# Three buffers for S1 in the seven-product matmul of a two-block layer, its loads and sums issued ahead, and S4 summed onto S2 in place

## The chip, the core and the metric

One core of a Trainium2 chip runs the whole program once. The time is device time in microseconds (us) of that one launch. TensorE is written PE, VectorE DVE, ScalarE ACT, GpSimd POOL, SyncE SP. SP and POOL issue the transfers that this text speaks of: SP the plain loads, POOL the loads that add onto what is in the buffer (an accumulating transfer), and the stores of the sigmoids.

## What is computed

A pooling block is followed by a layer with three attention branches. The change touches only two products of it: the gate logits (three matrices of 2048 x 2048, of which 42 of 48 tiles of 128 outputs are made in this way) and the last product with `w_out` (14 of its 16 tiles).

```python
def hybrid_layer(x, mem, ..., w_out):
    hn = rms_norm_2(x, norm_gain)
    proj = hn @ w_in                       # its last 3 * 2048 columns are gate_logits
    ...
    g = jax.nn.sigmoid(gate_logits.reshape(b, s, N_BRANCHES, D_MODEL))
    y = g[:, :, 0] * ua + g[:, :, 1] * ub + g[:, :, 2] * uc
    return x + y @ w_out
```

There are 512 tokens and 2048 features, all in float32.

## The kernel before

All activations lie feature by feature (128 partitions) with 512 tokens along the row. A float32 product is made of float32r parts: a weight tile is rounded to a high part by ACT (`pw_hi`, line 1496) and DVE takes the rest (`pw_lo`, line 2017); PE then multiplies high by high, high by low and low by high.

**Pairs.** The two stages that the change touches work on *pairs*: two output tiles of 128 features together. The weights of a pair are a 2 x 2 block matrix (two output tiles by the even and the odd feature tiles), and instead of eight block products seven are made (a Strassen-Winograd scheme), with these seven factors in this order:

| step o | factor | where it comes from |
|---|---|---|
| 0 | A11 | loaded by SP (line 985) |
| 1 | A12 | loaded by SP (line 997) |
| 2 | S2 | DVE: S1 + A11 (line 2028) |
| 3 | S1 | block (1,0) loaded by SP, the *base* (line 991), block (1,1) added onto it by a POOL transfer, the *sum* (line 2376) |
| 4 | S3 | base loaded by SP (line 1003), block (0,0) added by POOL (line 2381) |
| 5 | S4 | DVE: S2 + A12 (line 2031) |
| 6 | A22 | loaded by SP (line 1009) |

Each factor is 128 x 1024 float32, 512 KB, and has one buffer of 4 KB a partition in the space of `x3`. Seven of the eight such places are in use. One product (a step) is 16 matmuls, eight of 512 columns (line 1190) and eight of 256 (line 1192). There are 21 pairs for the gates (pairs 0 to 20, the *gate stage*) and 7 for the output (pairs 21 to 27, the *output stage*), with the attention and branch stages between.

**What sets the order.** Every engine's program is written out by hand and waits on semaphores. PE goes through the steps in order and waits at each for `pw_lo_ready`. ACT (`act_product`) and DVE (`dve_product`) work two steps ahead of PE: at step l, ACT and DVE convert the factor of step l+2, as the three buffers of `pw_hi` and `pw_lo` allow. DVE also makes the sums S2 and S4 four steps ahead (`weight_sum(f.ahead(4))`): at step 5 of a pair it adds one finished product (`added`), makes S2 of the *next* pair, and only then the low part of the next pair's A11:

```python
if f.o == 5:
    added(f, fifth_term, 3, chain[f.j])
    weight_sum(f.ahead(4))       # S2 of the next pair: waits s1_summed
...
factor_lo(f.ahead(2))            # A11 of the next pair
```

SP loads the factors of the next pair in the order A11, S1, A12, S3, A22, each when its single buffer has been read: S1 after `pw_lo` of the present pair's S1 (step 3, done by DVE at step 1), A12 after the present pair's S4 sum, S3 after `pw_lo` of S3. POOL does for each pair a sigmoid store, the sum onto S1, another sigmoid store, the sum onto S3, in that order (`gate_pair`). In the output stage POOL does only the two sums, and SP also loads `x_back` between the factors (`back_load`).

Of the kernel before, what the change touches and what calls it, by code (L numbers as in the profile page):

```python
# [6 lines left out]
F32 = mybir.dt.float32  # L7
# [5 lines left out]
P = 128  # L13
# [143 lines left out]
def program(nc, stream, wmod, cvec, xT, memT, cols_in, const_in, dist_in, x_store, c_store, mkv_store, sig_store, silu_store, out):  # L157
    ctx = ExitStack()
    with ctx:
# [13 lines left out]
        def sb(name, shape, dt, at):  # L173
# [20 lines left out]

        a11, s1, a12, s3, a22, s2, s4 = [sb(f"factor_{name}", [P, 8 * P], F32, at_x3 + 4 * KB * n) for n, name in
                                         enumerate(("a11", "s1", "a12", "s3", "a22", "s2", "s4"))]

# [710 lines left out]
        def _(sp):  # L908
# [66 lines left out]
            def load_factors(pair, which):  # L975

                first = pair.i is None and pair.c in (0, PAIRS)
                tiles = KT // 2 if pair.c == PAIRS else 0
                if "a11" in which:
                    if first:  # L980
                        sp.wait_ge(t_ready, tiles + 1)
                    else:
                        sp.wait_ge(pw_lo_ready, ((pair - 1).times(7) + 1).value())
                        sp.wait_ge(w_sum_made, (pair.times(2) - 1).value())
                    sp.dma_start(a11[:, :], block_in_stream(pair, 0, 0)).then_inc(a11_loaded, 16)
                if "s1" in which:
                    if first:
                        sp.wait_ge(t_ready, tiles + 2)
                    else:
                        sp.wait_ge(pw_lo_ready, ((pair - 1).times(7) + 4).value())  # L990
                    sp.dma_start(s1[:, :], block_in_stream(pair, 1, 0)).then_inc(s1_loaded, 16)
                if "a12" in which:
                    if first:
                        sp.wait_ge(t_ready, tiles + 3)
                    else:
                        sp.wait_ge(w_sum_made, pair.times(2).value())
                    sp.dma_start(a12[:, :], block_in_stream(pair, 0, 1)).then_inc(a12_loaded, 16)
                if "s3" in which:
                    if first:
                        sp.wait_ge(t_ready, tiles + 4)  # L1000
                    else:
                        sp.wait_ge(pw_lo_ready, ((pair - 1).times(7) + 5).value())
                    sp.dma_start(s3[:, :], block_in_stream(pair, 1, 0)).then_inc(s3_loaded, 16)
                if "a22" in which:
                    if first:
                        sp.wait_ge(t_ready, tiles + 5)
                    else:
                        sp.wait_ge(pw_lo_ready, ((pair - 1).times(7) + 7).value())
                    sp.dma_start(a22[:, :], block_in_stream(pair, 1, 1)).then_inc(a22_loaded, 16)
            every = ("a11", "s1", "a12", "s3", "a22")  # L1010
            load_factors(At(0), every)
            with steps(sp, 1, PAIRS) as i:
                load_factors(At(0, 1, i), every)
            sp.wait_ge(product_done, PRODUCTS - 2)
# [35 lines left out]
            for n in range(2):  # L1050
                back_load(n)
            load_factors(At(PAIRS), every)
            sp.wait_ge(xp_stored, 16 * (KT - 2))
            for p in range(OUT_PAIRS):
# [3 lines left out]
                if p + 1 < OUT_PAIRS:  # L1058
                    load_factors(At(PAIRS + p + 1), ("s1", "a12"))
                back_load(3 + 2 * p)  # L1060
                if p + 1 < OUT_PAIRS:
                    load_factors(At(PAIRS + p + 1), ("s3", "a22"))


# [180 lines left out]
        def _(act):  # L1245
# [227 lines left out]
            def factor_hi(f):  # L1473
# [19 lines left out]
                if (f.n - 2).positive():  # L1493
                    act.wait_ge(product_done, (f.n - 2).value())
                source = (a11, a12, s2, s1, s3, s4, a22)[f.o]
                nc.scalar.activation(pw_hi[f.slot][:, :], source[:, :], ACT.Copy).then_inc(pw_hi_ready, 1)  # L1496
# [177 lines left out]
        def _(dve):  # L1674
# [335 lines left out]
            def factor_lo(f):  # L2010

                dve.drain()
                if f is None:
                    return
                source = (a11, a12, s2, s1, s3, s4, a22)[f.o]
                dve.wait_ge(pw_hi_ready, (f.n + 1).value())
# [3 lines left out]
            def weight_sum(f):  # L2020
# [4 lines left out]
                if f.o == 2:  # L2025
                    dve.wait_ge(a11_loaded, once)
                    dve.wait_ge(s1_summed, once)
                    nc.vector.tensor_tensor(s2[:, :], s1[:, :], a11[:, :], ALU.add).then_inc(w_sum_made, 1)  # L2028
                else:
                    dve.wait_ge(a12_loaded, once)  # L2030
                    nc.vector.tensor_tensor(s4[:, :], s2[:, :], a12[:, :], ALU.add).then_inc(w_sum_made, 1)  # L2031

# [296 lines left out]
        def _(pool):  # L2329
# [43 lines left out]
            def sum_s1(pair):  # L2373

                pool.wait_ge(s1_loaded, (pair + 1).times(16).value())
                pool.dma_start(s1[:, :], block_in_stream(pair, 1, 1), accum_op=ALU.add).then_inc(s1_summed, 16)

# [5 lines left out]
            def gate_pair(q, i=None, sums=True):  # L2383

                pair = At(q, 3, i)
                if q or i:
                    n, b = At(2 + 2 * ((q - 1) // 3), 2, i), (q - 1) % 3
                    sigmoid_store(pair.times(2) + 1, n, b, 0)
                if sums:
                    sum_s1(pair + 1)  # L2390
                if q or i:
                    sigmoid_store(pair.times(2) + 2, n + 1, b, 1)
# [148 lines left out]
```

## Time and profile before

| | us |
|---|---|
| median of 3 runs (lowest to highest) | 2201.09 (2198.33 to 2208.2) |
| the profiled execution | 2200.44 |
| its span in the trace | 2198.9 |
| PE busy in the span | 2118.8 |
| DVE busy | 1594.6 |
| ACT busy | 972.5 |
| POOL busy | 126.4 |
| DVE's waits before S2 for the transfers of S1, 26 in all | 83.8 |
| PE's waits for `pw_lo`, 26 in all | 47.2 |

The profiled execution lies 0.65 us under the median of the runs, so what is read from the trace can be taken off the median as it stands. The ends of matmuls are modelled, and they overlap; how long a product takes is read from the start of its first matmul to the start of the next product's.

### The profile page before, as it was taken

What the parts mean: (1) busy time and instruction counts of PE and PEld (TensorE: products, weight loads), DVE (VectorE), ACT (ScalarE), POOL (GpSimd) and SP (SyncE); (2) the same over time, 40 slices, a digit from 0 to 9 for tenths busy, and PEclk for the clock granted to TensorE, in tenths of its full rate; (3) what the DMA queues carried; (4) which work ended last, traced back from release to release, by engine and by line L of the source; (5) the groups of instructions that cost most, each with busy time, mean ns of one, the idle gap of its engine ahead of it and who ended that gap; (6) DMA issues with size and microseconds to landing.
All of it is one profiled execution on the core that took longest, in us unless ns stands there. A gap on an engine that the chain in (4) does not pass through costs nothing.

```text
span 2198.9 us, 32924 instructions
## 1 busy us (share of the span) xinstructions
PE 2118.8 (96%) x10600; PEld 1758.8 (80%) x10600; DVE 1594.6 (73%) x2685; ACT 972.5 (44%) x1664; POOL 126.4 (6%) x201
## 2 busy tenths in 40 slices
PE   7899999999999899999999999999999999999898
PEld 6788887888887777777778878888787888888787
DVE  6888877675658677767676666666778776777676
ACT  6434454333335444444454444444545444224343
POOL 0000000000000111111110000000000000000000
PEclk9999999999999999999999999999999999999999
DMA  9767422655544667676764222222222224665775
GB/s 377 278 213 272 141 96 95 238 207 183 164 149 148 186 175 200 186 208 176 208 162 132 87 88 94 86 87 86 68 87 69 92 90 134 209 217 188 205 211 162
DMA packets 98026, 354.72 MB, mean 161 GB/s; under 512 B 11109, under 2 KB 13557, under 8 KB 89601
## 3 DMA queue, kind: packets, MB, share of 16 engines
q1 hardware_dynamic: 75600, 272.92, 37.4%
q0 software_dynamic: 19584, 76.04, 13.4%
q10 hardware_dynamic: 2738, 4.47, 0.5%
q8 instruction: 53, 0.87, 0.2%
q14 instruction: 51, 0.42, 0.1%
HBM read 328.45 MB, written 24.94 MB: 161 GB/s over the span
## 4 chain that ended last, share of the span: by engine, by line
PE 58%; DMA 15%; DVE 15%; DVEq 5%; ACT 4%; issue 3%; ACTq 0%; SPq 0%; POOLq 0%; POOL 0%
PE bank L427 18%; PE bank L429 17%; PE bank L428 17%; DMA factor_s<-stream 13%; DVE pw_lo L2017 5%; DVE w_lo L421 2%; PE bank L1190 2%; DVE factor_s L2028 1%; DVE factor_s L2031 1%; ACT w_hi L411 1%; PE bank L552 1%; PE bank L583 1%; DVEq L416 1%; DMA front_raw<-stream 1%; DVEq L2085 1%
## 5 line engine op out<-in xcount | busy, mean ns | idle before, releaser
L427 PE MATMUL bank<-x,w_hi 128*128 128x512 f32 x2000 | 789.4, 395 | 3.6 <-ACTq L1376 1.2
L429 PE MATMUL bank<-x,w_lo 128*128 128x512 f32 x2000 | 778.9, 389 | 0.0
L428 PE MATMUL bank<-x,w_hi 128*128 128x512 f32 x2000 | 778.8, 389 | 0.0
L1190 PE MATMUL bank<-x,pw_hi 128*128 128x512 f32 x1568 | 564.7, 404 | 51.1 <-DVE pw_lo L2017 47.2
L421 DVE TENSOR_TENSOR w_lo<-w_raw,w_hi 128x512 fp32r<-128x512 f32 x468 | 324.0, 692 | 315.6 <-ACT w_hi L411 284.2
L411 ACT ACTIVATE w_hi<-w_raw 128x512 fp32r<-128x512 f32 x468 | 295.9, 632 | 577.0 <-PE bank L429 475.6
L427 PEld LDWEIGHTS bank<-x,w_hi 128*128 128x128 f32 x2000 | 375.4, 188 | 95.5 <-issue 8.8
L1192 PE MATMUL bank<-x,pw_lo 128*128 128x256 f32 x1568 | 443.5, 283 | 0.0
L429 PEld LDWEIGHTS bank<-x,w_lo 128*128 128x128 f32 x2000 | 375.4, 188 | 79.7
L428 PEld LDWEIGHTS bank<-x,w_hi 128*128 128x128 f32 x2000 | 375.7, 188 | 75.3 <-issue 0.2
L1190 PEld LDWEIGHTS bank<-x,pw_hi 128*128 128x128 f32 x1568 | 300.0, 191 | 131.3 <-issue 30.7
L1192 PEld LDWEIGHTS bank<-x,pw_lo 128*128 128x128 f32 x1568 | 301.5, 192 | 0.0
L2017 DVE TENSOR_TENSOR pw_lo<-factor_s,pw_hi 128x1024 fp32r<-128x1024 f32 x112 | 137.2, 1225 | 32.7 <-ACT pw_hi L1496 21.1
L1496 ACT ACTIVATE pw_hi<-factor_s 128x1024 fp32r<-128x1024 f32 x112 | 118.9, 1062 | 40.0 <-PE bank L1192 18.9
L1496 ACT ACTIVATE pw_hi<-factor_a 128x1024 fp32r<-128x1024 f32 x84 | 89.1, 1061 | 80.4 <-PE bank L1192 72.1
L2017 DVE TENSOR_TENSOR pw_lo<-factor_a,pw_hi 128x1024 fp32r<-128x1024 f32 x84 | 102.9, 1225 | 24.9 <-ACT pw_hi L1496 17.4
L1692 DVE CUSTOM_DVE_ANT_0 wmod<-wmod,c_rows 128x2048 f32<-128x2048 f32 x48 | 109.7, 2286 | 0.0
L2028 DVE TENSOR_TENSOR factor_s<-factor_s,factor_a 128x1024 f32<-128x1024 f32 x28 | 34.3, 1225 | 83.8 <-DMA factor_s<-stream 83.8
L635 ACT ACTIVATE probs<-probs,neg_max 128x256 f32<-128x256 f32 (+3 forms) x112 | 57.1, 510 | 41.5 <-DVE neg_max L705 41.5
L411 ACT ACTIVATE w_hi<-front_raw 128x512 fp32r<-128x512 f32 x64 | 40.4, 632 | 66.3 <-PE bank L429 57.0
L421 DVE TENSOR_TENSOR w_lo<-front_raw,w_hi 128x512 fp32r<-128x512 f32 x64 | 44.3, 692 | 24.0 <-ACT w_hi L411 19.8
L1514 ACT ACTIVATE logits<-bank 128x256 f32<-128x256 f32 x21 | 8.1, 384 | 92.8 <-DVE second_sum L2036 85.6
(222 smaller groups left out, 1887.7 us busy)
## 6 DMA issues: line engine op xcount, KB each, us to landing
w_raw<-stream SPq DMA_DIRECT2D x234, 512.0 KB, 3.9
factor_a<-stream SPq DMA_DIRECT2D x84, 512.0 KB, 5.2
wmod<-w_mod_rows SPq DMA_DIRECT2D x32, 1024.0 KB, 6.7
factor_s<-stream SPq DMA_DIRECT2D x56, 512.0 KB, 4.4
factor_s<-stream POOLq DMA_DIRECT2D x56, 512.0 KB, 7.4
front_raw<-stream SPq DMA_DIRECT2D x16, 1024.0 KB, 9.1
wmod<-w_mod_rows POOLq DMA_DIRECT2D x16, 1024.0 KB, 5.5
sig_store<-logits POOLq DMA_DIRECT2D x45, 256.0 KB, 4.7
```

The source lines that it names most:

```text
L411: nc.scalar.activation(w_hi[:, q, :], raw_quarter(s), ACT.Copy).then_inc(hi_ready, 1)
L421: nc.vector.tensor_tensor(w_lo[:, q, :], raw_quarter(s), w_hi[:, q, :].bitcast(F32), ALU.subtract).then_inc(lo_ready, 1)
L427: nc.tensor.matmul(bank_ap[:, :tokens], hi, x_hi[:, kx, :], start=start, stop=False)
L428: nc.tensor.matmul(bank_ap[:, :tokens], hi, x_lo[:, kx, :], start=False, stop=False)
L429: return nc.tensor.matmul(bank_ap[:, :tokens], lo, x_hi[:, kx, :], start=False, stop=stop)
L635: nc.scalar.activation(seg, seg, ACT.Exp, bias=neg_max[:, k:k + 1], scale=-1.0, accum_out=den[:, k:k + 1]).then_inc(exp_done, 1)
L1190: nc.tensor.matmul(to[:, :].rearrange("p (a t) -> p a t", a=2), hi, x[:, :, 2 * k + odd, tokens], start=begins, stop=False, skip_group_che ...
L1192: mm = nc.tensor.matmul(to[:, :HALF], lo, x[:, 0, 2 * k + odd, tokens], start=False, stop=k == 7, skip_group_check=True)
L1496: nc.scalar.activation(pw_hi[f.slot][:, :], source[:, :], ACT.Copy).then_inc(pw_hi_ready, 1)
L1692: nc.vector.tensor_tensor_reduce(out=wmod_sb[slot][:, :], in0=wmod_sb[slot][:, :], in1=c_rows[:, :], scale=1.0, scalar=0.0, op0=ALU.mult, ...
L2017: nc.vector.tensor_tensor(pw_lo[f.slot][:, :], source[:, :], pw_hi[f.slot][:, :].bitcast(F32), ALU.subtract).then_inc(pw_lo_ready, 1)
L2028: nc.vector.tensor_tensor(s2[:, :], s1[:, :], a11[:, :], ALU.add).then_inc(w_sum_made, 1)
```

## The change

S1 gets three buffers, used in turn by pair number modulo 3. Two of them are new: one is the eighth place in `x3`, the other is the place of S4, which is now written over S2. SP's list for a pair becomes S1, A11, A12, S3, A22, where the S1 base stands in front of the rest and is the S1 of the same pair as the A11 behind it; A12 now waits for `pw_lo` of the last pair's S3, and S3 waits only for its own pair's S1 base (which stands before it in the queue). The S1 base of pair 1, and that of pair 22, is issued in the start of its stage, behind A22 of the first pair. On POOL the sum onto the next pair's S1 moves ahead of both sigmoid stores, and waits also until the S1 sum before it has landed.

```diff
-        a11, s1, a12, s3, a22, s2, s4 = [sb(f"factor_{name}", [P, 8 * P], F32, at_x3 + 4 * KB * n) for n, name in
-                                         enumerate(("a11", "s1", "a12", "s3", "a22", "s2", "s4"))]
+        a11, s1_0, a12, s3, a22, s2_s4, s1_1, s1_2 = [
+            sb(f"factor_{name}", [P, 8 * P], F32, at_x3 + 4 * KB * n) for n, name in
+            enumerate(("a11", "s1_0", "a12", "s3", "a22", "s2_s4", "s1_1", "s1_2"))]
+        s1 = [s1_0, s1_1, s1_2]
...
                     else:
                         sp.wait_ge(pw_lo_ready, ((pair - 1).times(7) + 1).value())
-                        sp.wait_ge(w_sum_made, (pair.times(2) - 1).value())
+                        if pair.i is None:
+                            sp.wait_ge(w_sum_made, (pair.times(2) - 1).value())
                     sp.dma_start(a11[:, :], block_in_stream(pair, 0, 0)).then_inc(a11_loaded, 16)
-                if "s1" in which:
...
-                        sp.wait_ge(pw_lo_ready, ((pair - 1).times(7) + 4).value())
-                    sp.dma_start(s1[:, :], block_in_stream(pair, 1, 0)).then_inc(s1_loaded, 16)
                 if "a12" in which:
...
-                        sp.wait_ge(w_sum_made, pair.times(2).value())
+                        sp.wait_ge(pw_lo_ready, ((pair - 1).times(7) + 5).value())
...
                 if "s3" in which:
...
-                        sp.wait_ge(pw_lo_ready, ((pair - 1).times(7) + 5).value())
+                        sp.wait_ge(s1_loaded, (pair + 1).times(16).value())
...
-            every = ("a11", "s1", "a12", "s3", "a22")
-            load_factors(At(0), every)
-            with steps(sp, 1, PAIRS) as i:
-                load_factors(At(0, 1, i), every)
+            def load_s1(pair, j, tile=None):
+
+                if tile is not None:
+                    sp.wait_ge(t_ready, tile)
+                else:
+                    sp.wait_ge(pw_lo_ready, ((pair - 3).times(7) + 4).value())
+                sp.dma_start(s1[j][:, :], block_in_stream(pair, 1, 0)).then_inc(s1_loaded, 16)
+            every = ("a11", "a12", "s3", "a22")
+            load_factors(At(0), ("a11",))
+            load_s1(At(0), 0, 2)
+            load_factors(At(0), ("a12", "s3", "a22"))
+            sp.wait_ge(s1_loaded, 16)
+            load_s1(At(1), 1, 7)
+            load_factors(At(1), every)
+            load_s1(At(2), 2, 8)
+            load_factors(At(2), every)
+            with steps(sp, 1, PAIRS // 3) as i:
+                for j in range(3):
+                    load_s1(At(j, 3, i), j)
+                    load_factors(At(j, 3, i), every)
...
-            load_factors(At(PAIRS), every)
+            load_factors(At(PAIRS), ("a11",))
+            load_s1(At(PAIRS), 0, KT // 2 + 2)
+            load_factors(At(PAIRS), ("a12", "s3", "a22"))
+            sp.wait_ge(s1_loaded, 16 * (PAIRS + 1))
+            load_s1(At(PAIRS + 1), 1, KT // 2 + 7)
...
                 if p + 1 < OUT_PAIRS:
-                    load_factors(At(PAIRS + p + 1), ("s1", "a12"))
+                    load_factors(At(PAIRS + p + 1), ("a12",))
                 back_load(3 + 2 * p)
                 if p + 1 < OUT_PAIRS:
                     load_factors(At(PAIRS + p + 1), ("s3", "a22"))
+                if p + 2 < OUT_PAIRS:
+                    load_s1(At(PAIRS + p + 2), (p + 2) % 3, KT // 2 + 8 if p == 0 else None)
...
-                    nc.vector.tensor_tensor(s2[:, :], s1[:, :], a11[:, :], ALU.add).then_inc(w_sum_made, 1)
+                    nc.vector.tensor_tensor(s2_s4[:, :], s1[f.j][:, :], a11[:, :], ALU.add).then_inc(w_sum_made, 1)
...
-                    nc.vector.tensor_tensor(s4[:, :], s2[:, :], a12[:, :], ALU.add).then_inc(w_sum_made, 1)
+                    nc.vector.tensor_tensor(s2_s4[:, :], s2_s4[:, :], a12[:, :], ALU.add).then_inc(w_sum_made, 1)
...
                 pool.wait_ge(s1_loaded, (pair + 1).times(16).value())
-                pool.dma_start(s1[:, :], block_in_stream(pair, 1, 1), accum_op=ALU.add).then_inc(s1_summed, 16)
+                if pair.positive():
+                    pool.wait_ge(s1_summed, pair.times(16).value())
+                pool.dma_start(s1[pair.c % 3][:, :], block_in_stream(pair, 1, 1), accum_op=ALU.add).then_inc(s1_summed, 16)
...
             def gate_pair(q, i=None, sums=True):
 
                 pair = At(q, 3, i)
+                if sums:
+                    sum_s1(pair + 1)
                 if q or i:
                     n, b = At(2 + 2 * ((q - 1) // 3), 2, i), (q - 1) % 3
                     sigmoid_store(pair.times(2) + 1, n, b, 0)
-                if sums:
-                    sum_s1(pair + 1)
-                if q or i:
                     sigmoid_store(pair.times(2) + 2, n + 1, b, 1)
```

The order of instructions on PE, ACT and DVE stays as it is. On SP, in the loop over the pairs of the gate stage, one pass stood like this (a pass is a pair; `factor_a11` and the like are the buffers, a row with `ISA` is a wait):

```order
L984 ISA [waits pw_lo_ready]
L985 ISA [waits w_sum_made]
L985 DMA factor_a11_61<-stream 128x1024
L990 REGISTER_ALU
L991 ISA [waits pw_lo_ready]
L991 DMA factor_s1_62<-stream 128x1024
L997 ISA [waits w_sum_made]
L997 DMA factor_a12_63<-stream 128x1024
L1002 REGISTER_ALU
L1003 DMA factor_s3_64<-stream 128x1024 [waits pw_lo_ready]
L1009 ISA [waits pw_lo_ready]
L1009 DMA factor_a22_65<-stream 128x1024
```

and in the changed kernel the first of the three pairs of a pass stands like this:

```order
L1013 ISA [waits pw_lo_ready]
L1013 DMA factor_s1_0_62<-stream 128x1024
L985 REGISTER_ALU
L988 ISA [waits pw_lo_ready]
L988 DMA factor_a11_61<-stream 128x1024
L993 REGISTER_ALU
L994 ISA [waits pw_lo_ready]
L994 DMA factor_a12_63<-stream 128x1024
L999 ISA
L1000 DMA factor_s3_64<-stream 128x1024 [waits s1_base_loaded]
L1006 ISA [waits pw_lo_ready]
L1006 DMA factor_a22_65<-stream 128x1024
```

The S1 base has moved from between A11 and A12 to the front, that is, right behind the A22 of the pair before, and A12 and S3 go out together.

On POOL, in the loop of the gate stage, one pair stood like this (`sig_store` is the store of a row of sigmoids, `logits0` and `logits1` its two buffers):

```order
L2370 REGISTER_ALU
L2371 ISA [waits sigmoid_made]
L2371 DMA sig_store<-logits0_112 128x512
L2375 REGISTER_ALU
L2376 ISA [waits s1_base_loaded]
L2376 DMA factor_s1_62<-stream 128x1024
...
L2371 DMA sig_store<-logits1_113 128x512
L2381 ISA [waits s3_base_loaded]
L2381 DMA factor_s3_64<-stream 128x1024
```

and in the changed kernel like this:

```order
L2394 REGISTER_ALU
L2397 ISA [waits s1_summed,s1_base_loaded]
L2397 DMA factor_s1_0_62<-stream 128x1024
L2389 REGISTER_ALU
L2390 ISA [waits sigmoid_made]
L2390 DMA sig_store<-logits0_113 128x512
...
L2390 DMA sig_store<-logits1_114 128x512
L2402 ISA [waits s3_base_loaded]
L2402 DMA factor_s3_64<-stream 128x1024
```

The S1 sum now stands ahead of both stores, right behind the S3 sum of the pair before.

## Rows read from the trace of the kernel before

**Rows 1.** Stretches of the span: busy us (instructions) of each engine, granted PE clock, DMA share, GB/s.
```profile
702.00:1164.00 462.00, 425.75 (x2357) 365.20 (x2357) 334.97 (x383) 221.98 (x272) 59.30 (x83) 0.98 0.68 186
904.00:910.00 6.00, 6.00 (x26) 5.15 (x27) 5.26 (x7) 2.65 (x4) 0.00 (x0) 0.72 0.39 113
2036.00:2198.00 162.00, 144.37 (x788) 123.95 (x787) 113.84 (x130) 64.66 (x74) 11.20 (x13) 0.97 0.70 193
```

**Rows 2.** Timeline of PE: start us, us, instruction, [idle before <- releaser]; gate stage.
```profile
702.75 0.47 PE L1190 MATMUL bank<-x,pw_hi 128*128 128x512 f32 x1
...
885.22 0.39 PE L1190 MATMUL bank<-x,pw_hi 128*128 128x512 f32 x1
...
899.09 0.39 PE L1190 MATMUL bank<-x,pw_hi 128*128 128x512 f32 x1
...
903.85 0.49 PE L1190 MATMUL bank<-x,pw_hi 128*128 128x512 f32 x1 [1.83 <-DVE pw_lo L2017]
...
908.31 0.40 PE L1190 MATMUL bank<-x,pw_hi 128*128 128x512 f32 x1
...
922.44 0.40 PE L1190 MATMUL bank<-x,pw_hi 128*128 128x512 f32 x1
...
1163.44 0.28 PE L1192 MATMUL bank<-x,pw_lo 128*128 128x256 f32 x1
```

**Rows 3.** Timeline of PE, output stage.
```profile
2036.73 0.39 PE L1190 MATMUL bank<-x,pw_hi 128*128 128x512 f32 x1
...
2043.52 0.50 PE L1190 MATMUL bank<-x,pw_hi 128*128 128x512 f32 x1 [3.82 <-DVE pw_lo L2017]
...
2195.14 0.28 PE L1192 MATMUL bank<-x,pw_lo 128*128 128x256 f32 x1
```

**Rows 4.** Who waited for whom, whole span: us in total, times, longest us.
```profile
DVE factor_s L2028 <- DMA factor_s<-stream: 83.8, 26, 4.5
...
PE bank L1190 <- DVE pw_lo L2017: 47.2, 26, 3.8
```

**Rows 5.** Timeline of DVE around one pair's end.
```profile
901.11 1.23 DVE L2028 TENSOR_TENSOR factor_s<-factor_s,factor_a 128x1024 f32<-128x1024 f32 x1 [3.13 <-DMA factor_s<-stream]
...
915.98 1.23 DVE L2017 TENSOR_TENSOR pw_lo<-factor_s,pw_hi 128x1024 fp32r<-128x1024 f32 x1 [1.51 <-ACT pw_hi L1496]
...
923.45 1.23 DVE L2028 TENSOR_TENSOR factor_s<-factor_s,factor_a 128x1024 f32<-128x1024 f32 x1 [2.23 <-DMA factor_s<-stream]
```

**Rows 6.** Timeline of SP's transfer issues in the same pair.
```profile
890.23 0.33 SPq L991 DMA_DIRECT2D factor_s<-stream  x1
...
892.84 0.33 SPq L1003 DMA_DIRECT2D factor_s<-stream  x1
896.97 0.33 SPq L1009 DMA_DIRECT2D factor_a<-stream  x1
```

**Rows 7.** Line 1003, the loads of the S3 base (28).
```profile
DMA to landing us min/median/max: 4.0/4.5/8.3
```

**Rows 8.** Line 2376, the S1 sums (28 of them).
```profile
DMA to landing us min/median/max: 5.4/6.5/10.1
```

**Rows 9.** Timeline of DVE in pair 0: the fold that waits for a sigmoid store.
```profile
721.84 0.43 DVE L2051 TENSOR_TENSOR logits<-first_term 128x256 f32<-128x256 f32 x1 [4.47 <-DMA sig_store<-logits]
```

**Rows 10.** Line 997, the loads of A12 (28).
```profile
DMA to landing us min/median/max: 4.2/5.1/7.5
```

**Rows 11.** The costliest groups, page: engine, tiles, xcount | busy us, mean ns | idle before, releaser.
```profile
L2017 DVE TENSOR_TENSOR pw_lo<-factor_s,pw_hi 128x1024 fp32r<-128x1024 f32 x112 | 137.2, 1225 | 32.7 <-ACT pw_hi L1496 21.1
L1496 ACT ACTIVATE pw_hi<-factor_s 128x1024 fp32r<-128x1024 f32 x112 | 118.9, 1062 | 40.0 <-PE bank L1192 18.9
```

**Rows 12.** Timeline of POOL, the S3 sum of the same pair.
```profile
897.54 0.88 POOL L2381 DMA_DIRECT2D factor_s<-stream  x1 [1.10 <-DMA factor_s<-stream]
```

**Rows 13.** Line 2381, the S3 sums (28).
```profile
DMA to landing us min/median/max: 5.9/8.5/9.7
```

**Rows 14.** Line 2059, a DVE product written over its own operand: ns min/median/max.
```profile
L2059 DVE TENSOR_TENSOR logits<-logits,r_both x42: 691/692/694, 729.4 to 1166.9; 128x512 f32<-128x512 f32 x42
```

More of the change, by code:

```diff
@@ L983, in load_factors @@
                         sp.wait_ge(pw_lo_ready, ((pair - 1).times(7) + 1).value())
-                        sp.wait_ge(w_sum_made, (pair.times(2) - 1).value())
+                        if pair.i is None:
+                            sp.wait_ge(w_sum_made, (pair.times(2) - 1).value())
                     sp.dma_start(a11[:, :], block_in_stream(pair, 0, 0)).then_inc(a11_loaded, 16)
-                if "s1" in which:
-                    if first:
-                        sp.wait_ge(t_ready, tiles + 2)
-                    else:
-                        sp.wait_ge(pw_lo_ready, ((pair - 1).times(7) + 4).value())
-                    sp.dma_start(s1[:, :], block_in_stream(pair, 1, 0)).then_inc(s1_loaded, 16)
                 if "a12" in which:
@@ L1494, in factor_hi @@
                     act.wait_ge(product_done, (f.n - 2).value())
-                source = (a11, a12, s2, s1, s3, s4, a22)[f.o]
+                source = (a11, a12, s2_s4, s1[f.j], s3, s2_s4, a22)[f.o]
                 nc.scalar.activation(pw_hi[f.slot][:, :], source[:, :], ACT.Copy).then_inc(pw_hi_ready, 1)
@@ L2014, in factor_lo @@
                     return
-                source = (a11, a12, s2, s1, s3, s4, a22)[f.o]
+                source = (a11, a12, s2_s4, s1[f.j], s3, s2_s4, a22)[f.o]
                 dve.wait_ge(pw_hi_ready, (f.n + 1).value())
```

## The prediction

> **What bounds the kernel now.** I read first the stretches of the span, to see where PE is not fed. In the attention and branch stages between the two pair stages nothing changes. In the gate stage PE is busy 425.75 of 462 us, in the output stage 144.37 of 162, and in both its clock is a little under full: 0.98 and 0.97 of it [rows 1]. Only these two stretches can change.
>
> Next the timeline of PE, for what a product costs when nothing stops it. Between 885.22 and 899.09 lie five products, 2.77 us each; between 908.31 and 922.44 five more, 2.83 each [rows 2]. A pair runs at one or the other, and I take 2.80. At the pair's end the seventh product starts at 899.09 and the next pair's first at 903.85: 4.76 us, of which some 2 are a stall, and the row says that PE waited for DVE's low part of A11. That first product then takes 4.46 us (to 908.31), because the clock granted after the stall fell: 0.72 over those six microseconds, which is a mix of the lower level (1.2 GHz) and the full 2.4 [rows 1, 2].
>
> So I have the price of the stage. The gate stage runs from 702.75 to 1163.44, 460.7 us, and its 147 products at 2.80 are 411.6: **49.1 us over**. The output stage runs from 2036.73 to 2195.14, 158.4 us, its 49 products are 137.2: **21.2 over** [rows 2, 3].
>
> Then who waited for whom. PE waited 47.2 us for `pw_lo` in 26 places, and DVE 83.8 us, also in 26 places, at S2 for a transfer into an S1 buffer [rows 4]. These are one thing: DVE stands at S2 of the next pair, and the low part of A11, for which PE waits, is behind it in DVE's program. In the pair shown, S2 starts at 901.11 after 3.13 us of waiting [rows 5]. SP issued that S1's base at 890.23 [rows 6], when DVE had read the single buffer; base, POOL's issue and sum took the 10.9 us between. From this S2 to the next (923.45) DVE's own work is 22.34 less its two waits of 1.51 and 2.23, that is 18.6 us [rows 5]. PE needs 7 x 2.80 = 19.6. So neither DVE nor PE sets the pair's length but the ring S1 read, base, sum, S2, which has one buffer.
>
> **The change, part by part.**
>
> *S1 ahead.* The base of S1 now goes out right behind A22. In the pair shown A22 goes at 896.97 [rows 6]; half a microsecond later, by SP's 0.33 for an issue and its waits, leaves the base for the S2 of 923.45, which before left only after DVE had read the S1 of 901.11. The base of S3, as large, lands in 4.5 us, at most 8.3 [rows 7]; the sum lands 6.5 us after its issue, at most 10.1 [rows 8]. That is 908.8 with the medians, 916 with the slowest. S2 is wanted when DVE comes to it, at 923.45 - 2.23 = 921.2 [rows 5], and with PE never stopped some 3.6 us earlier (this pair's stall of 2.0 and its slow product's 1.7). It is there by 9 us, at worst by 1.6. I take the wait at S2 as gone, 26 of 26.
>
> *What is given back.* Of the gate stage all 49.1 us: 20 boundaries, and in pair 0 the stall behind DVE's fold, which waited 4.47 us for a sigmoid store [rows 9]. That store stood on POOL behind the sum onto pair 1's S1, whose base could only leave when pair 0's S1 was read; now that base leaves before pair 0 starts. Of the output stage the start stays: its first product is followed by 6.79 us instead of 2.80 (2036.73 to 2043.52) [rows 3], and one more product at the low clock costs 1.6 like the one above, 5.6 together, since pair 21's first S1 can't be loaded before its place is free. 21.2 - 5.6 = 15.6. **Together 64.7 us.**
>
> *A12 later.* It goes out with S3, after `pw_lo` of S3 (892.84 in the pair shown, rather than right behind S1 at 890.23). It lands in 5.1 us, at most 7.5 [rows 10]: 897.9, or 900.3. ACT has a free buffer for it from 899.09, when the seventh product starts, and PE wants it two products on, at 904.7; the conversions take 1.06 and 1.23 us [rows 11], so ACT may begin as late as 902. Cost 0; if the cover failed, each microsecond past 902 would be one for PE in each pair.
>
> *S3.* Its loop becomes the next shortest: read, A12 and S3 issued (0.6), base 4.5, POOL 0.2 (897.54 is 4.7 after 892.84), sum 8.5, conversions 1.06 + 1.23 and three handovers of 0.1: 16.4 us against 19.6 [rows 6, 7, 11 to 13]. Covered by 3.2 us; with the slowest base and sum (8.3 and 9.7) it is 21.4 and not covered.
>
> *DVE and ACT.* The same instructions. S4 over S2 in place: a DVE product over its own operand at half the width takes 692 ns, beside 1225 for the full width out of place [rows 11, 14], so I take 0; were it slower by a tenth that would be 0.1 x 28, under 3, on DVE alone, and it could gain no more. DVE at 18.6 of 19.6 us is close: what is late next is any step in which it waits for ACT or a transfer. I allow 0.2 us of stall a boundary, 26 x 0.2 = 5.2; its ends are 0 and 0.8, some two fifths of what the boundary shown loses now, and I stay near 0 as DVE gains a microsecond on PE in each pair.
>
> *The starts.* In pairs 0 and 21 the extra base (of S1 for the next pair) now runs beside the first sum, which S2 waits for. A sum takes between 5.4 and 10.1 us by what is beside it [rows 8], so each costs 0 to 3.6; I take 1 each, 2 together. The transfers use 0.68 of the engines over a pair of 22 us [rows 1], 15 us' worth; over 19.6 that is 0.76. That leaves room, and I take landing times as they are. If all landing times grew as the share does, by 0.76/0.68, S3's loop would be 18 us and the sum would stand. The Trainium skill ("DMA: Bandwidth & Descriptors", section "Issuing engines are not separate DMA queues") speaks against such a change: transfers of SP and POOL run on the same 16 DMA engines and interleave, so issuing earlier adds no bandwidth. By the rows the sum is the one below; by the rule taken to its end, transfers side by side each taking the time of both, it would be that of the third rival.
>
> **Sum:** 64.7 - 5.2 - 2 = 57.5 us off. From the median 2201.09 (the profiled execution, 2200.44, is 0.65 under it) this gives 2143.6; I say **2143**.
>
> **Rivals.**
>
> *S3's sum binds in S1's place.* If S3's loop comes to 20.6 us instead of 16.4, a microsecond a boundary stays: 26 less is gained, 2143 + 26 - 5 = 2164; at 21.4 it is 1.8, 2143 + 47 - 5 = 2185. For it: A12 now goes out beside S3's base and the next S1 base behind A22. Against it: S3's base was not alone before either, and no step waited for the S3 sum. Chance 0.14.
>
> *It does not do what it says.* The base of S1 stands in SP's queue behind A22, so it leaves four steps earlier and no more; if the sum still came after DVE wanted S2, nothing would change: 2201. It would have to land 9 us later than reckoned above. Chance 0.04.
>
> *Slower: the two sums side by side on POOL.* S1's sum now follows S3's of the pair before, and if each took the time of both (6.5 + 8.5 = 15), S3's loop would be 16.4 + 6.5 = 22.9 us against the 21.9 a pair takes now (460.7/21); 26 boundaries by 22.9 - 19.6 = 3.3 is 86 us on the 2138 that no stall would give: 2224. It decides from an S3 sum of 14 us on. The interleaving of which the Trainium skill speaks in the section named above would make it. Against it: S1's and S3's sums overlap now too, and S3's never took over 9.7 [rows 13]. Chance 0.05.
>
> **How the numbers follow.** My case has 0.77. Its own ends: all products at 2.77 instead of 2.80 (196 x 0.03 = 5.9 less), no stall (5.2) and no loss at the starts (2) give 2130; all at 2.83 (5.9 more) and 0.8 a boundary (15.6 more) give 2165. The range 2130 to 2166 holds most of my case (0.72) and the nearer half of the first rival (0.08): 0.8. A measurement tells about 0.5%, 11 us, from no change. Faster by more than that is my case and the first rival, 0.91; within it the second, 0.04; slower the third, 0.05.
>
> **What would show it.** DVE's wait at S2 for a transfer should all but vanish from the waits (83.8 us now), PE's for `pw_lo` fall from 47.2 to under 12, the pairs start 19.4 to 20 us apart, the granted clock be 1.00 in the gate stage, and pair 0's sigmoid store cost no wait. If a wait of ACT for an S3 buffer appears, the first rival is at work; if POOL's sums take 12 us and more, the third; if S2 still waits, the second. I am wrong if pairs are over 20.3 us apart, whatever the reason.

## The result, and the profile after

The changed kernel takes **2138.38 us** (median of four runs, 2135.98 to 2140.62), the one before on the same chip 2202.92: a ratio of 0.9706, 95% interval [0.9681, 0.9732], 64.5 us less. The forecast was 2143, with a range of 2130 to 2166. The execution profiled is the one of 2135.98 us; its span is 2134.4.

First the stretches, as in [rows 1]: busy us (instructions) of PE, PE's weight loads, DVE, ACT and POOL, then the granted PE clock, the DMA share and GB/s. The first row is the gate stage, the last the output stage.

```profile
702.00:1117.00 415.00, 415.00 (x2349) 359.60 (x2348) 331.95 (x380) 221.04 (x270) 59.99 (x83) 1.00 0.78 206
1117.00:1989.00 872.00, 867.98 (x4322) 706.02 (x4321) 622.82 (x1336) 378.90 (x823) 28.04 (x51) 1.00 0.35 113
1989.00:2134.00 145.00, 139.21 (x798) 121.11 (x796) 115.28 (x132) 65.83 (x75) 11.24 (x13) 1.00 0.80 219
```

In the gate stage PE is busy for all of its 415 us at a clock of 1.00, where it was busy 425.75 of 462 at 0.98. The transfers use 0.78 of the DMA engines instead of 0.68.

Then PE's timeline: the first matmul of the gate stage, of pairs 10 and 11, and the stage's last; below them the start of pair 21, its second product, the start of pair 22, and the last matmul.

```profile
702.97 0.47 PE L1209 MATMUL bank<-x,pw_hi 128*128 128x512 f32 x1
...
900.87 0.40 PE L1209 MATMUL bank<-x,pw_hi 128*128 128x512 f32 x1
...
920.65 0.40 PE L1209 MATMUL bank<-x,pw_hi 128*128 128x512 f32 x1
...
1118.40 0.28 PE L1211 MATMUL bank<-x,pw_lo 128*128 128x256 f32 x1
...
1991.85 0.39 PE L1209 MATMUL bank<-x,pw_hi 128*128 128x512 f32 x1
...
1997.58 0.49 PE L1209 MATMUL bank<-x,pw_hi 128*128 128x512 f32 x1 [2.75 <-DVE pw_lo L2036]
...
2014.32 0.39 PE L1209 MATMUL bank<-x,pw_hi 128*128 128x512 f32 x1
...
2130.68 0.28 PE L1211 MATMUL bank<-x,pw_lo 128*128 128x256 f32 x1
```

The gate stage lasts 415.4 us (702.97 to 1118.40) instead of 460.7 [rows 2], the output stage 138.8 instead of 158.4 [rows 3]: 45.3 and 19.6 given back, together 64.9. Pairs 10 and 11 stand 19.78 apart, and so do all pairs of the stage within 0.1; none of the 20 boundaries has a stall. One is left in the two pair stages, 2.75 us at the second product of pair 21.

Who waited for whom, over the whole span (us in total, times, longest), beside [rows 4]:

```profile
ACT pw_hi L1515 <- DMA factor_s<-stream: 5.8, 3, 2.8
...
DVE factor_s_s L2047 <- DMA factor_s<-stream: 3.3, 2, 3.0
...
PE bank L1209 <- DVE pw_lo L2036: 2.8, 1, 2.8
```

DVE's 83.8 us at S2 are 3.3, PE's 47.2 for `pw_lo` are 2.8. New is the first row: ACT waits for the S3 sum in three places (in pairs 2, 21 and 22), where it never did before; behind none of them does PE stop. Next one pair on SP, POOL and DVE (three timelines): SP's issues of A12, S3's base, A22 and the S1 base of pair 11, then POOL's S1 sum, then the S2 that uses it.

```profile
890.36 0.33 SPq L994 DMA_DIRECT2D factor_a<-stream  x1
890.88 0.33 SPq L1000 DMA_DIRECT2D factor_s<-stream  x1
895.81 0.33 SPq L1006 DMA_DIRECT2D factor_a<-stream  x1
896.41 0.33 SPq L1013 DMA_DIRECT2D factor_s<-stream  x1
...
903.51 0.87 POOL L2397 DMA_DIRECT2D factor_s<-stream  x1 [5.71 <-DMA factor_s<-stream]
...
916.52 1.22 DVE L2047 TENSOR_TENSOR factor_s_s<-factor_s,factor_a 128x1024 f32<-128x1024 f32 x1
```

S2 at 916.52 waits for nothing. Last, the landings of the lines: S1's base, S1's sum, S3's base, S3's sum.

```profile
DMA to landing us min/median/max: 4.8/6.7/10.0
...
DMA to landing us min/median/max: 5.4/7.2/9.3
...
DMA to landing us min/median/max: 4.5/5.8/8.8
...
DMA to landing us min/median/max: 7.1/8.8/10.2
```

S1's sum, issued at 903.51, is there by 910.7 with the median: 5.8 us before S2. The transfers are slower than before, where S3's base took 4.5, S1's sum 6.5 and S3's sum 8.5 [rows 7, 8, 13].

### The profile page after: what moved, and what is told of

It reads as the page before. It is cut to its first block, busy times and chain, and to the rows that moved or that the text cites. A ratio compares the mean times of both kernels' runs of the same rounds, so it can differ in the third digit from the quotient of the medians.

```text
span 2134.4 us, 32913 instructions
## 1 busy us (share of the span) xinstructions
PE 2103.3 (99%) x10600; PEld 1750.8 (82%) x10600; DVE 1593.0 (75%) x2685; ACT 974.4 (46%) x1664; POOL 127.4 (6%) x201
## 3 DMA queue, kind: packets, MB, share of 16 engines
q10 hardware_dynamic: 2738, 4.47, 0.6%
## 4 chain that ended last, share of the span: by engine, by line
PE 84%; DVE 6%; ACT 4%; DVEq 3%; DMA 2%; issue 1%; ACTq 0%; SPq 0%
PE bank L429 18%; PE bank L431 18%; PE bank L430 18%; PE bank L1209 17%; PE bank L1211 9%; DVE w_lo L423 2%; ACT w_hi L413 1%; PE bank L554 1%; PE bank L585 1%; DVEq L418 1%; DMA front_raw<-stream 1%; PE bank L567 1%; ACT probs L637 1%; DMA factor_s<-stream 1%; DMA mem_raw<-mem_features 0%
## 5 line engine op out<-in xcount | busy, mean ns | idle before, releaser
L1209 PE MATMUL bank<-x,pw_hi 128*128 128x512 f32 x1568 | 551.7, 397 | 2.8 <-DVE pw_lo L2036 2.8
L1211 PE MATMUL bank<-x,pw_lo 128*128 128x256 f32 x1568 | 438.9, 280 | 0.0
L1209 PEld LDWEIGHTS bank<-x,pw_hi 128*128 128x128 f32 x1568 | 294.5, 188 | 75.5 <-DVE pw_lo L2036 3.1
L1211 PEld LDWEIGHTS bank<-x,pw_lo 128*128 128x128 f32 x1568 | 295.7, 189 | 0.0
L2036 DVE TENSOR_TENSOR pw_lo<-factor_s_s,pw_hi 128x1024 fp32r<-128x1024 f32 x56 | 68.6, 1226 | 44.8 <-ACT pw_hi L1515 40.3
L2036 DVE TENSOR_TENSOR pw_lo<-factor_s,pw_hi 128x1024 fp32r<-128x1024 f32 x56 | 68.6, 1226 | 8.2 <-issue 3.3
L1515 ACT ACTIVATE pw_hi<-factor_s 128x1024 fp32r<-128x1024 f32 x56 | 59.5, 1063 | 24.1 <-PE bank L1211 14.1
L1515 ACT ACTIVATE pw_hi<-factor_s_s 128x1024 fp32r<-128x1024 f32 x56 | 59.5, 1063 | 16.3 <-DVE factor_s_s L2047 8.4
```

The lines of the kernel that those rows point to most:

```text
L1209: nc.tensor.matmul(to[:, :].rearrange("p (a t) -> p a t", a=2), hi, x[:, :, 2 * k + odd, tokens], start=begins, stop=False, skip_group_che ...
L1211: mm = nc.tensor.matmul(to[:, :HALF], lo, x[:, 0, 2 * k + odd, tokens], start=False, stop=k == 7, skip_group_check=True)
L2036: nc.vector.tensor_tensor(pw_lo[f.slot][:, :], source[:, :], pw_hi[f.slot][:, :].bitcast(F32), ALU.subtract).then_inc(pw_lo_ready, 1)
```

## The experiments

My theory: only the moment at which S1's base leaves SP counts, since the ring from the reading of S1 over base and sum to the next S2 was the bound. Rivals: POOL's new order carries the gain; the third buffer or S4 in place carries it; a part of a pair's lead would do; S3's loop is now close behind. Ratios below are to the kernel before on the same chip.

**POOL's order back.** The sum onto S1 stands behind the first sigmoid store again.

```diff
-                if sums:
-                    sum_s1(pair + 1)
                 if q or i:
                     ...
                     sigmoid_store(pair.times(2) + 1, n, b, 0)
+                if sums:
+                    sum_s1(pair + 1)
+                if q or i:
                     sigmoid_store(pair.times(2) + 2, n + 1, b, 1)
```

> The change with POOL's old order alone put back: the sum onto the next S1 stands behind the first sigmoid store again, no longer ahead of it. Theory (what counts is when S1's base leaves SP; POOL's order is not needed): in the trace of after the store goes at 907.00, so the sum would leave at 907.3 instead of 903.51 and land 7.2 later at 914.5, still 2 us ahead of the S2 of 916.52: 2138, at most 2148 for the slowest sums (9.3); DVE's wait at S2 under 15 in all. Rival (the new order on POOL carries the gain): most of it is lost, 2180 to 2203, and DVE waits 50 us or more at S2 again.

Measured 2137.84 us, ratio 0.9724 [0.9692, 0.9756]; DVE waits 0.4 us at S2 in the gate stage. POOL's timeline shows the sum 4 us later than in the changed kernel:

```profile
906.80 0.56 POOL L2390 DMA_DIRECT2D sig_store<-logits  x1 [7.62 <-ACT logits L1520]
907.57 0.88 POOL L2397 DMA_DIRECT2D factor_s<-stream  x1 [0.21 <-issue]
```

and DVE's timeline the S2 that uses it, without a wait:

```profile
916.37 1.22 DVE L2047 TENSOR_TENSOR factor_s_s<-factor_s,factor_a 128x1024 f32<-128x1024 f32 x1
```

This part of the change is worth nothing by itself: S2 came 8.8 us after the sum was issued, and sums took 5.7 (median).

**S1's base at its old place; then A12 too.** The first kernel keeps the three places, S4 in place and the later A12, and loads in the order A11, S1, A12, S3, A22; the second puts A12 back as well. S3 waits for the low part of the last S3, as before, and POOL has its old order.

```diff
-                    load_s1(At(j, 3, i), j)
                     load_factors(At(j, 3, i), every)
...
+                if "s1" in which:
+                        sp.wait_ge(pw_lo_ready, ((pair - 1).times(7) + 4).value())
+                    sp.dma_start(s1[pair.c % 3][:, :], block_in_stream(pair, 1, 0)).then_inc(s1_loaded, 16)
```
```diff
-                        sp.wait_ge(pw_lo_ready, ((pair - 1).times(7) + 5).value())
+                        sp.wait_ge(w_sum_made, pair.times(2).value())
                     sp.dma_start(a12[:, :], block_in_stream(pair, 0, 1)).then_inc(a12_loaded, 16)
```

> Everything of the change (three S1 buffers, S4 in place, A12 later) but S1's base back between A11 and A12 of its own pair, after the low part of S1 of the pair before, and POOL's order back. Theory (the ring S1 read, base, sum, S2 is what bound, and the early issue alone opens it): the time of before, 2203 (2190 to 2215), DVE waiting about 84 us at S2 in 26 places, pairs 21 to 23 us apart. Rival (the third buffer, S4 in place or the later A12 give a part of the gain by themselves): 2138 to 2180.

> The kernel with S1's base at its old place (2216 us), with A12's load also back at its old place: of the change only the three places for S1 and S4 added in place are left. Theory (buffers and in place are worth nothing by themselves; that run was 13 us over the kernel before since A12 and S3 then ran beside S1's sum, 7.3 us rather than 6.5): 2200 (2193 to 2207), S1's sum back at 6.5. Rival (S4 in place, or the turn of buffers, costs those 13 us): 2210 to 2220.

Measured 2216.07, ratio 1.0081 [1.0049, 1.0113], and 2201.43, ratio 1.0002 [0.998, 1.0024]. The waits at S2 for the transfer are back, the first row of the one kernel, the second of the other:

```profile
DVE factor_s_s L2036 <- DMA factor_s<-stream: 82.8, 26, 4.8
```
```profile
DVE factor_s_s L2036 <- DMA factor_s<-stream: 78.3, 27, 4.7
```

So the whole gain hangs on the earlier base, and the buffers alone give 0. That three buffers are needed for it, and two would not do, no run shows. The first result was just outside what I had written (2190 to 2215), and the second says why: the later A12, free in the changed kernel, costs some 15 us where S1's sum is on the path. With it the sum took 7.3 us, without it 6.5.

**One step earlier, and no more.** S1's base as in the first of these two, but after the low part of S2 instead of S1's; then the same with A12 back; then with S3's base one step later besides.

```diff
-                        sp.wait_ge(pw_lo_ready, ((pair - 1).times(7) + 4).value())
+                        sp.wait_ge(pw_lo_ready, ((pair - 1).times(7) + 3).value())
                     sp.dma_start(s1[pair.c % 3][:, :], block_in_stream(pair, 1, 0)).then_inc(s1_loaded, 16)
```
```diff
-                        sp.wait_ge(pw_lo_ready, ((pair - 1).times(7) + 5).value())
+                        sp.wait_ge(pw_lo_ready, ((pair - 1).times(7) + 6).value())
                     sp.dma_start(s3[:, :], block_in_stream(pair, 1, 0)).then_inc(s3_loaded, 16)
```

> As the kernel before it in this call, but S1's base one step of DVE earlier: after the low part of S2 of the pair before instead of S1's. Theory (a ring with a length: 21.9 us a pair in before, a step is 2.8, so 19.1 against PE's 19.8): nearly all of the gain is there already, 2140 to 2155; pairs 19.8 to 20.3 apart, and what stays comes from slow landings. Rival (a whole pair ahead is needed, as base and sum are slow beside the other loads): 2165 to 2190, DVE waiting over 40 us at S2.

Measured 2178.4, ratio 0.9913 [0.988, 0.9945]: the rival's number. One ring of this kernel, from S2 to S2, on DVE, SP, POOL and DVE:

```profile
890.03 1.23 DVE L2036 TENSOR_TENSOR factor_s_s<-factor_s,factor_a 128x1024 f32<-128x1024 f32 x1 [0.97 <-DMA factor_s<-stream]
...
897.90 0.33 SPq L994 DMA_DIRECT2D factor_s<-stream  x1
...
903.95 0.88 POOL L2386 DMA_DIRECT2D factor_s<-stream  x1 [4.11 <-DMA factor_s<-stream]
...
912.55 1.23 DVE L2036 TENSOR_TENSOR factor_s_s<-factor_s,factor_a 128x1024 f32<-128x1024 f32 x1 [3.71 <-DMA factor_s<-stream]
```

From S2 to the issue of the base it is 7.87 us. In the kernel before it was 10.77, from the S2 at 901.11 [rows 5] to this issue on SP's timeline:

```profile
911.88 0.33 SPq L991 DMA_DIRECT2D factor_s<-stream  x1
```

The step of 2.9 is there. But base and sum take 14.65 (897.90 to 912.55) instead of 11.57 (911.88 to the S2 at 923.45), so that this ring is 22.5 again, as it was 22.3. The medians of the landings say the same more mildly: base 4.7 instead of 4.3, sum 8.0 instead of 6.5. The ring shown is one of the long ones: 6 of the 20 pairs before the gate stage's last take 19.4 to 19.8 us here, as in the changed kernel. I had taken the ring for a length; it is a length that depends on what runs beside it.

> The kernel with S1's base one step earlier (2178 us), with A12's load back at its old place. Theory (the step of 2.9 was given back by landings: base 4.7 and sum 8.0 where 4.3 and 6.5 were, since A12, S3's base and its sum run beside S1's sum; A12 earlier ends before the sum begins): sum at 7 or under, 2150 to 2168. Rival (any load as early as this one takes as long, whatever A12 does): 2172 to 2185, sum still 7.5 to 8.

Measured 2172.3, ratio 0.9859 [0.9814, 0.9903], sum 8.2: the rival. A12 was not what slowed this sum.

> The kernel with S1's base one step earlier and A12 back (2172 us, S1's sum 8.2 us), with S3's base one step later, so that it is issued some 3 us into S1's sum and no more right behind its start, as in the kernel before (there S3's base went 2 us ahead of the sum, and the sum took 6.5). Theory (which load starts beside S1's sum sets how long the ring is; S3's base, issued 0.9 us behind it, is the one that made it 8.2): sum 7.3 or under, 2145 to 2162. Rival (a sum in that part of the pair takes 8 us whichever load is beside it): 2166 to 2182, sum 7.8 to 8.6.

Measured 2161.94, ratio 0.9811 [0.979, 0.9832], at the upper edge of the theory. The landings of S1's sum, A12 back (first) and S3's base later besides (second):

```profile
DMA to landing us min/median/max: 6.5/8.2/9.5
```
```profile
DMA to landing us min/median/max: 5.4/6.6/10.5
```

With this one wait moved, 13 of the 20 pairs before the gate stage's last take 19.4 to 19.9 us; the others still stop. The issues of all 20 S1 sums and S3 bases of the gate stage put the kernels in one line (median distance from the sum's issue to that of S3's base, median landing of the sum over all 28):

| kernel | S3's base after the sum, us | S1's sum lands in, us |
|---|---|---|
| before; buffers alone | -2.3; -2.3 | 6.5; 6.5 |
| old place, later A12 | -1.2 | 7.3 |
| one step earlier, A12 back | 0.5 | 8.2 |
| one step earlier | 1.1 | 8.0 |
| one step earlier, A12 back, S3's base later | 2.4 | 6.6 |
| the change with POOL's order back | 2.9 | 5.7 |

The sum takes 0.8 to 1.7 us more than the 6.5 of the kernel before where S3's base starts between 1.2 ahead of it and 1.1 behind it, and no more in the two kernels where the base starts 2.4 and 2.9 behind. Only the pair with A12 back, without and with S3's base later (0.5 and 2.4 in the table), differs in that one wait; it shows that the base's moment, with the S3 sum that follows it, makes the 1.6 us there. The other rows agree, but in them more than the base has moved.

The line does not go on. In the kernels with S1 a pair ahead and POOL's new order, S3's base goes 4.7 to 9 us after the sum, and the sum still takes 6.6 to 7.3. In the changed kernel (6.9 after, 7.2) other transfers are beside it: A11, issued 4.2 us ahead of the sum and landed 2.9 us after its issue, and mostly the S3 sum of the pair before, landed 2.3 us after. With POOL's order back alone the sum leaves 4 us later, when both have mostly landed, and takes 5.7. That these two make the difference is argued from this, not shown. The Trainium skill says in "DMA: Bandwidth & Descriptors", section "Issuing engines are not separate DMA queues", that transfers started by ScalarE, SyncE or GpSimd run on the same 16 DMA engines and interleave: these sums, from POOL, slowed by a base from SP, agree with it.

**S3's base one step later, in the changed kernel.** SP waits with it for the low part of S4. (That S1's base has landed, for which S3 waited, the next S1 base waits for here and in the next kernel.)

```diff
-                        sp.wait_ge(s1_loaded, (pair + 1).times(16).value())
+                        sp.wait_ge(pw_lo_ready, ((pair - 1).times(7) + 6).value())
                     sp.dma_start(s3[:, :], block_in_stream(pair, 1, 0)).then_inc(s3_loaded, 16)
```

> The change with S3's base one step later: after the low part of S4 instead of S3's of the pair before. Theory (S3's loop is the next shortest, and with the landings that after shows, 5.8 and 8.8 where 4.5 and 8.5 were reckoned, it is 18.0 us a pair; a step more is 20.8 against PE's 19.8): a microsecond in 26 places, 2164 (2150 to 2178), with ACT waiting for the S3 sum and PE behind it. Rival (it is 16.4 as reckoned before the change, or DVE's lead over PE takes it up): 2138 to 2145.

Measured 2138.45, ratio 0.972 [0.9687, 0.9752]: no change, the theory of this run fell. With landings of 5.1 and 8.5 here, the loop with its extra step is 0.6 + 2.8 + 5.1 + 0.2 + 8.5 + 2.6 = 19.8 us, PE's own length. ACT now waits for the S3 sum in 8 places of the gate stage, and none of it reaches PE there (the row is of the gate stage alone):

```profile
ACT pw_hi L1515 <- DMA factor_s<-stream: 13.0, 8, 2.4
```

S3 has a step in hand, and by this row no more.

**A12 back, in the changed kernel.** The second diff of the old-place kernels; S3's base then waits itself for the low part of the last S3, as A12 no longer does so ahead of it.

> The change with A12's load at its old place in time (after the sum S4 of the pair before rather than after the low part of S3, some 2 us earlier). Theory (A12's later load costs nothing, and with S1 a pair ahead its earlier one gains nothing): 2138 (2133 to 2144), pairs 19.8 us apart, S1's sum landing in 6.5 to 8 us. Rival (the later A12 is what keeps the loads out of each other's way): S1's or S3's sum takes 9 us and more and S2 or the conversion of S3 waits, 2150 to 2175.

Measured 2133.02 (2128.23 to 2138.03), ratio 0.9679 [0.9634, 0.9723], pairs 19.79 apart and S1's sum at 7.3: the later A12 costs nothing and gains nothing here.

**Pauses of PE.** In the profiles of the first three kernels with S1 a pair ahead, every product of the gate stage took 2.83 us, while in the output stage it was 2.77 or 2.83. To see what sets that pace, PE pauses ahead of pairs.

```diff
                 if f.o == 0 and (pair - 2).positive():
                     pe.wait_ge(row_read, (pair - 2).times(4).value())
+                    pe.wait_ge(term_copied, pair.times(4).value())
```

> The change with a pause of PE put in: the first product of each pair waits for ACT's copy of the chain of the pair before, so PE is drained and idle for about a microsecond in 25 places. A look at the two paces of the products, 2.77 and 2.83 us. Theory (a pace is taken up when PE starts again after a pause and held until the next one, whatever the stage): both paces among the pairs of each stage, each constant inside its pair; 2138 + 25 x 1 to 1.5 = 2163 to 2178. Rival (the pace belongs to the stage, by its loads or operands): 2.83 in all 21 pairs of the gate stage, as in three profiles of unpaused kernels.

One run, 2160.02 us. PE's timeline at the starts of pairs 3, 4 and 5, with a matmul five products on in the first two:

```profile
762.65 0.47 PE L1210 MATMUL bank<-x,pw_hi 128*128 128x512 f32 x1 [0.65 <-ACT logits L1534]
...
765.51 0.39 PE L1210 MATMUL bank<-x,pw_hi 128*128 128x512 f32 x1
...
779.38 0.39 PE L1210 MATMUL bank<-x,pw_hi 128*128 128x512 f32 x1
...
782.87 0.50 PE L1210 MATMUL bank<-x,pw_hi 128*128 128x512 f32 x1 [0.55 <-ACT logits L1534]
785.78 0.40 PE L1210 MATMUL bank<-x,pw_hi 128*128 128x512 f32 x1
...
799.92 0.40 PE L1210 MATMUL bank<-x,pw_hi 128*128 128x512 f32 x1
...
803.46 0.50 PE L1210 MATMUL bank<-x,pw_hi 128*128 128x512 f32 x1 [0.55 <-ACT logits L1534]
```

Pair 3 runs at (779.38 - 765.51) / 5 = 2.774 us, pair 4 at (799.92 - 785.78) / 5 = 2.828. Pairs 0 to 3 run at the shorter pace, pairs 4 to 20 and all of the output stage at the longer. The pace doesn't belong to the stage, it changed only at a pause, and inside a pair it never changes: so far the theory. Both paces in each stage did not come: after 17 of the 18 pauses of the gate stage, and in all of the output stage, it was the longer. What decides is not shown. A pause cost less than I had put: PE idles 0.47 to 0.65 us for the copy, a pair is 20.6 long instead of 19.8.

A pause need not show as idle time of PE. In the last of the kernels with S1's base one step earlier (A12 back, S3's base later), the seven products before 785.88 run at 2.83 and the six behind it at 2.77, and the row at the change has no idle time. DVE's row below shows the low part that this product needs: it ended at 785.65, 0.12 us ahead of the product's first weight load. Pair 16 of the kernel with A12 back alone is another such case.

```profile
766.09 0.40 PE L1198 MATMUL bank<-x,pw_hi 128*128 128x512 f32 x1
...
785.88 0.39 PE L1198 MATMUL bank<-x,pw_hi 128*128 128x512 f32 x1
...
802.53 0.39 PE L1198 MATMUL bank<-x,pw_hi 128*128 128x512 f32 x1
...
784.43 1.22 DVE L2025 TENSOR_TENSOR pw_lo<-factor_a,pw_hi 128x1024 fp32r<-128x1024 f32 x1 [0.16 <-ACT pw_hi L1504]
```

Where PE does idle for `pw_lo` at the start of a pair in these kernels, the low part ends 0.05 to 0.13 us ahead of that load; in the changed kernel it ends 0.8 us and more ahead, in all pairs that follow another.

**The start of pair 21.** S1's base is issued ahead of A11 in pairs 0 and 21 (they change places in memory), and DVE makes the low part of A12 before pair 21's S2.

```diff
-            load_factors(At(PAIRS), ("a11",))
-            load_s1(At(PAIRS), 0, KT // 2 + 2)
+            load_s1(At(PAIRS), 0, KT // 2 + 1)
+            load_factors(At(PAIRS), ("a11",))
...
-                    weight_sum(Factor(PRODUCTS + 2))
                     factor_lo(Factor(PRODUCTS + 1))
                     token_sums_lo(KT - 1)
+                    weight_sum(Factor(PRODUCTS + 2))
+                    dve.drain()
```

> The change, with the start of pairs 0 and 21 put in another order: S1's base is issued ahead of A11 (they change places in memory, so it has the place that comes free first), and at pair 21 DVE makes the low part of A12 before it waits for S1's sum. Theory (the one stall left, 2.75 us of PE at pair 21, is that sum's landing): the stall goes to 0 to 1.3, 2136 (2128 to 2140), faster than before by the whole of the change and at best 2 to 3 us more. Rival (A11, now issued 2 us later, is late instead, or the stall only moves to the third product): stall 2 to 4 us at another place, 2136 to 2142.

Measured 2133.93 (2128.5 to 2136.32), ratio 0.968 [0.9658, 0.9702]. PE at pair 21's start, the two moments of this pair in which it idles by 0.2 us or more, and pair 22's start:

```profile
1991.57 0.39 PE L1209 MATMUL bank<-x,pw_hi 128*128 128x512 f32 x1
...
1997.78 0.47 PE L1209 MATMUL bank<-x,pw_hi 128*128 128x512 f32 x1 [0.40 <-issue]
...
2003.85 0.50 PE L1209 MATMUL bank<-x,pw_hi 128*128 128x512 f32 x1 [0.28 <-DVE pw_lo L2036]
...
2012.28 0.40 PE L1209 MATMUL bank<-x,pw_hi 128*128 128x512 f32 x1
```

Pair 21 takes 20.71 us instead of 22.47: 1.8 us gained, and of the stall of 2.75 us the two short ones of 0.40 and 0.28 are left. It is the fastest version here by the trace; by the runs' times its interval overlaps that of the change alone.

## Why the prediction was right

**The bound was the one named.** The ring through S1's single buffer set the pair's length: with its base at the old place nothing of the change is left (2201.43), with it a pair ahead every boundary is closed. The signs came: pairs 19.4 to 19.8 apart (but for pair 21, whose start was reckoned apart), a clock of 1.00, no stall in pair 0, where DVE's fold had waited 4.47 us for a store [rows 9]. One sign of the first rival came too, ACT's 5.8 us of waits for the S3 sum, without the cost to PE that the rival says.

**The sum, term by term.** Gate stage: forecast 49.1 less 20 boundaries at 0.2 and 1 for the start, 44.1; measured 45.3. The allowance and the start were not needed, and the pace took 3.8 back, since all 147 products ran at 2.83 and not at 2.80. Output stage: forecast 15.6 less 6 x 0.2 and 1, 13.4; measured 19.6. Pair 21's start keeps 3.1 us (22.47 less seven products of 2.77) and not 6.6: its S2 waited 2.95 us instead of 3.99, and no slow product followed. The slower second product did come there in two of the other profiles (4.45 and 4.46 us, where this one has 2.88), so that this is worth 1.6 either way from run to run. Allowance (1.2) and pace (1.3) make up the rest. Together 64.9 came back where 57.5 was forecast: 5.2 for stalls that don't occur and 4.5 at the two starts, less 2.5 for the pace. The output stage's pace and the slow product differ from profile to profile, and the pace cancelled a part of the caution; that the forecast came within 5 us is in part luck. The closed boundaries, 20 and 6, are not.

**S1's lead** was reckoned at 9 us and is 5.8, as base and sum take 6.7 and 7.2 and not 4.5 and 6.5. I wrote that I take landing times as they are; that step was too kind, and it did not show as the lead was wide. The same error made the expectation of the kernel one step earlier wrong by 23 us and more: there the lead was narrow.

**DVE's own work** is less than the 18.6 us that I read from S2 to S2. This row of the same stretch has a third wait, for ACT, so that 17.9 is left:

```profile
918.81 1.23 DVE L2017 TENSOR_TENSOR pw_lo<-factor_a,pw_hi 128x1024 fp32r<-128x1024 f32 x1 [0.73 <-ACT pw_hi L1496]
```

That gives DVE 1.7 us in hand against PE's 19.6 and not 1.0, in line with no stall at any boundary.

**A12, S4 in place, S3, POOL.** A12's later load costs 0, confirmed by putting it back. S4 takes 1225 ns over its own operand (min/median/max in the rows of its line), as it did out of place:

```profile
L2050 DVE TENSOR_TENSOR factor_s_s<-factor_s_s,factor_a x28: 1224/1225/1227, 708.5 to 2114.9; 128x1024 f32<-128x1024 f32 x28
```

S3's loop, forecast 16.4, is 18.0 with the landings of after (0.6 + 5.8 + 0.2 + 8.8 + 2.6), still under 19.8, so the first rival cost nothing; the second fell with the waits at S2; no S3 sum took over 10.2, far from the 14 of the third. The Trainium skill's rule that the prediction named, on interleaving transfers, is in the landings, as slower loads, and not in the time.

## What to carry to other kernels

When an engine waits for a load whose buffer is read late, look at the ring of that buffer, and give the load a whole turn's lead rather than the few microseconds that the wait shows: here the landings moved by up to 2.4 us with what ran beside them (S1's base from 4.3 to 6.7, its sum from 6.5 to 8.2), which takes a narrow lead away again. A part of a change that costs nothing beside a wide lead (the later A12) costs 15 us where the lead is missing, so parts are judged in the kernel they stand in. And an allowance for stalls at each boundary wants a row with a second wait that ends as late; here there was none, and the 5.2 us allowed were not needed.

## What was not expected of the hardware

The same 16 matmuls run at 2.77 or at 2.83 us, and in these traces keep the one or the other until PE has to wait, if only for so short a time that no idle time shows: 147 products at 2.83 in the changed kernel, 8 us more than at 2.77, with the granted clock at 1.00 in both. What decides is open; a profile shows one run, so how far it makes the spread of the runs (2128 to 2142 us over all kernels with S1 a pair ahead and no pauses) wasn't tried.
